# Five tiles' convolution taps on TensorE in four phases, instead of four tiles in two

## What is computed

```python
def conformer_conv_module(x, norm_g, pw1_w, pw1_b, dw_w, dw_b, ln_g, ln_b, pw2_w, pw2_b):
    h = rms_norm(x, norm_g)
    u = h @ pw1_w + pw1_b
    u = u[..., :D_MODEL] * jax.nn.sigmoid(u[..., D_MODEL:])
    u = causal_depthwise_conv(u, dw_w, dw_b)          # 31 taps, each channel by itself
    u = jax.nn.silu(layer_norm(u, ln_g, ln_b))
    return x + u @ pw2_w + pw2_b
```

## Time and profile before

| | us |
|---|---|
| median of 3 runs | 1212.82 |
| lowest, highest | 1211.44, 1214.83 |
| the profiled execution | 1212.73 |
| its span in the profile | 1211.0 |

### The profile page before, as it was taken

The page is one execution under the profiler, slowest core; times in us unless marked ns, Lnnn a source line. Parts: engine busy times, 40 slices in busy tenths (PEclk is TensorE's granted clock), DMA queues, the critical chain, the costliest instruction groups (busy, mean ns, idle before and its releaser), DMA issues.

```text
span 1211.0 us, 16270 instructions
## 1 busy us (share of the span) xinstructions
PE 1188.5 (98%) x6026; PEld 997.4 (82%) x6026; DVE 799.1 (66%) x1099; ACT 506.5 (42%) x814; POOL 62.7 (5%) x76
## 2 busy tenths in 40 slices
PE   8999969999999999999999999999999999999998
PEld 6888838888888888887899999987788888888887
DVE  6998946577527763576667786876677446753763
ACT  6331245444314341334656656655444224421441
POOL 1000001100000000001222021200000000000000
PEclk9999989999999999999999999999999999999999
DMA  8564711232323223222322211231233323332222
GB/s 291 152 125 114 198 46 38 102 100 79 129 76 104 87 89 117 90 87 87 105 71 71 70 42 65 71 105 35 70 104 104 104 70 104 104 104 79 94 78 95
DMA packets 34613, 116.75 MB, mean 96 GB/s; under 512 B 18304, under 2 KB 18432, under 8 KB 21888
## 3 DMA queue, kind: packets, MB, share of 16 engines
q1 hardware_dynamic: 34560, 116.03, 30.3%
HBM read 109.60 MB, written 6.49 MB: 96 GB/s over the span
## 4 chain that ended last, share of the span: by engine, by line
PE 90%; DVE 5%; ACT 3%; issue 1%; DMA 1%; POOL 0%; SPq 0%; POOLq 0%; DVEq 0%; ACTq 0%
PE bank L1240 71%; PE bank L1397 8%; PE bank L1313 5%; PE bank L1447 1%; PE bank L1431 1%; DVE w_lo L839 1%; PE bank L1334 1%; ACT prob L793 1%; PE bank L1304 1%; DVE small L1164 1%; PE bank L1279 1%; DVE dT_lo L1156 1%; DMA w_raw<-stream 1%; PE bank L1416 0%; DVE w_lo L831 0%
## 5 line engine op out<-in xcount | busy, mean ns | idle before, releaser
L1240 PE MATMUL bank<-xg_hi,w_hi 128*128 128x512 f32 x832 | 326.7, 393 | 2.3 <-DVE xg_lo L847 2.3
L1240 PE MATMUL bank<-xg_lo,w_hi 128*128 128x512 f32 x832 | 323.8, 389 | 0.0
L1240 PE MATMUL bank<-xg_hi,w_lo 128*128 128x512 f32 x832 | 323.8, 389 | 0.0
L556 ACT ACTIVATE w_hi<-w_raw 128x2048 fp32r<-128x2048 f32 x79 | 150.6, 1907 | 149.0 <-PE bank L1240 147.1
L831 DVE TENSOR_TENSOR w_lo<-w_raw,w_hi 128x2048 fp32r<-128x2048 f32 x79 | 182.7, 2312 | 31.0 <-ACT w_hi L556 31.0
L1240 PEld LDWEIGHTS bank<-xg_hi,w_hi 128*128 128x128 f32 x832 | 156.2, 188 | 37.0 <-DVE xg_lo L847 2.4
L1240 PE MATMUL bank<-act_hi,w_hi 128*128 128x512 f32 x448 | 177.1, 395 | 7.5 <-DVE act_lo L984 7.2
L708 ACT ACTIVATE ffn_t<-ffn_u,par 128x512 f32<-128x512 f32 x88 | 72.0, 818 | 268.7 <-DVE ffn_u L1054 268.7
L1240 PEld LDWEIGHTS bank<-xg_lo,w_hi 128*128 128x128 f32 x832 | 156.2, 188 | 33.9 <-issue 1.7
L1240 PEld LDWEIGHTS bank<-xg_hi,w_lo 128*128 128x128 f32 x832 | 156.1, 188 | 32.3
L1240 PE MATMUL bank<-act_hi,w_lo 128*128 128x512 f32 x448 | 175.2, 391 | 0.0
(11 more groups left out here) (159 smaller groups left out, 1418.5 us busy)
## 6 DMA issues: line engine op xcount, KB each, us to landing
w_raw<-stream SPq DMA_DIRECT2D x87, 1024.0 KB, 4.9
band_sb<-band SPq DMA_DIRECT2D x12, 512.0 KB, 6.6
w_raw<-stream SPq DMA_DIRECT2D x8, 768.0 KB, 4.1
band<-band_sb SPq DMA_DIRECT2D x4, 1056.0 KB, 12.1
x<-x_t SPq DMA_DIRECT2D x8, 256.0 KB, 6.6
w_raw<-band SPq DMA_DIRECT2D x4, 512.0 KB, 5.8
out_t<-x SPq DMA_DIRECT2D x8, 256.0 KB, 2.0
w_raw<-stream SPq DMA_DIRECT2D x2, 512.0 KB, 5.0
```

The lines of the kernel that those rows point to most:

```text
L556: act.activation(w_hi[:, j, :], w_raw[:, j, :], ACT.Copy).then_inc(w_hi_done, 1)
L1240: got = pe.matmul(out, weights(w, j, k, m), v[:, k, :], start=(k == first and s == 0), stop=(k == last and s == 2), skip_group_check=True)
```

## The change

- **Tiles.** DVE convolves tiles 0 to 2, PE tiles 3 to 7.
- **Phases.** 4 instead of 2: a band is 32 channels by 4 phases, 9 matmuls (OFFSETS) of 128x128, weights 128x1152 (576 KB). There are 20 bands. ACT makes `u2` with 16 copies of 32 partitions by 135 or 136 a tile, and copies a band out with four copies of 32x128.
- **Band rows.** No zero fill of DRAM and no scatter by element. DVE reduces the identity matrix to `taken` (32 columns, which channel of its group a partition is) and makes each tile's rows, 128x992, as tap times `taken` (`make_band`): tiles' rows 0 and 1 in step m = 0 of the pw1 loop, 2 and 3 in m = 1, 4 in m = 2. They go to one of three drafts in SBUF, are stored in DRAM (624 KB, `store_band`), then copied from DRAM to DRAM, four copies of 576 KB a tile, 128 rows of 4608 bytes each (`copy_bands`), and each band is then one load over 128 partitions (`load_band`).
- **Homes.** 13 bands have a place of their own: 3 in `band_sb`, 3 in `w_raw` (free once unit 7 is split), 7 in `xg_band`, which lies over pw1's activations (free when pw1 is done). 7 more reuse places.
- **Queue.** SP's order is new (below), as are the places in which units 8 and 9 are loaded and split.
- **Mean.** DVE adds tiles 0 to 6 into `sq_sum`; PE makes two matmuls with ones instead of eight, one before the last band and one after it.

```diff
-DVE_TILES = [0, 1, 2, 3]
-PE_TILES = [4, 5, 6, 7]
-PHASES = 2
+DVE_TILES = [0, 1, 2]
+PE_TILES = [3, 4, 5, 6, 7]
+PHASES = 4
+CH = P // PHASES
...
+            def store_band(tile):
+                sp.wait_ge(band_made, tile + 1)
+                sp.dma_start(bass.AP(band.tensor, tile * P * BAND, [[BAND, P], [1, BAND]]), drafts[:, tile % DRAFTS, :]
+                             ).then_inc(band_set[tile], 16)
...
+            def copy_bands(tile):
+                sp.wait_ge(band_set[tile], 16)
                 for r in range(PHASES):
...
+                    sp.dma_start(bass.AP(band_rows.tensor, (tile * PHASES * P + r * CH) * BAND_COLS,
+                                         [[BAND_COLS, CH], [P * BAND_COLS, PHASES], [1, BAND_COLS]]),
+                                 bass.AP(band.tensor, tile * P * BAND + r * CH, [[BAND, CH], [CH * BAND, PHASES], [1, BAND_COLS]])
+                                 ).then_inc(band_copied[tile], 16)
+
+            def load_unit(n):
+                sp.wait_ge(w_lo_done, n - RING + 1)
+                sp.dma_start(w_raw[:, n % RING, :], stream[:, STARTS[n]:STARTS[n + 1]]).then_inc(w_in[n % RING], 16)
+
+            load_unit(2)
+            load_unit(3)
+            load_unit(4)
+            store_band(0)
+            store_band(1)
+            copy_bands(0)
+            load_unit(5)
+            copy_bands(1)
+            store_band(2)
+            store_band(3)
+            copy_bands(2)
+            copy_bands(3)
+            load_unit(6)
+            store_band(4)
+            copy_bands(4)
+            load_unit(7)
+            for n in range(HOMES):
+                if n % PHASES == 0:
+                    sp.wait_ge(band_copied[n // PHASES], 16 * PHASES)
+                if n == SB_BANDS:
+                    sp.wait_ge(w_lo_done, KT)
+                if n == SB_BANDS + RAW_BANDS:
+                    sp.wait_ge(tiles, TILE0 + 2 * KT)
                 load_band(n)
...
+            def make_band(tile):
+                dve.wait_ge(taken_set, 1)
+                dve.wait_ge(band_edges, 2)
+                if tile >= DRAFTS:
+                    dve.wait_ge(band_set[tile - DRAFTS], 16)
+                dve.tensor_tensor(drafts[:, tile % DRAFTS, BAND_AT:BAND_AT + TAPS * CH].rearrange("p (t c) -> p t c", c=CH),
+                                  p("dw_w", PE_TILES[tile] * TAPS, TAPS).rearrange("p (t c) -> p t c", c=1).broadcast_to([P, TAPS, CH]),
+                                  taken.rearrange("p (t c) -> p t c", t=1).broadcast_to([P, TAPS, CH]),
+                                  ALU.mult).then_inc(band_made, 1)
...
+                for tile in {0: (0, 1), 1: (2, 3), 2: (4,)}.get(m, ()):
+                    make_band(tile)
                 convolve(4)
                 if 0 < m < KT - 2:
                     split_weights(m + 2, j)
...
-            convolve(12)
-            split_weights(KT + 1, 1)
-            convolve(len(taps))
+            dve.wait_ge(c_done, len(DVE_TILES))
+            for n in range(KT - 2):
+                if n:
+                    dve.wait_ge(conv_summed, n)
+                if n + 1 in PE_TILES:
+                    dve.wait_ge(band_out, PHASES * (n + 2 - PE_TILES[0]))
+                if n == len(DVE_TILES) + 1:
+                    split_weights(KT + 1, 1)
+                dve.tensor_tensor(sq_sum, sq_sum if n else conv_c[:, 0, :], conv_c[:, n + 1, :], ALU.add).then_inc(conv_summed, 1)
```

More of the change, by code:

```diff
@@ L52 @@
 CHUNKS = [KT, KT, FT - 2 * KT]
-DVE_TILES = [0, 1, 2, 3]
-PE_TILES = [4, 5, 6, 7]
-PHASES = 2
+DVE_TILES = [0, 1, 2]
+PE_TILES = [3, 4, 5, 6, 7]
+PHASES = 4
+CH = P // PHASES
+OFFSETS = (TAPS + PHASES - 2) // PHASES + 1
+BAND_COLS = OFFSETS * P
+BAND = (OFFSETS * PHASES + PHASES - 1) * CH
+PHASE_SEQ = SEQ // PHASES
+PHASE_COLS = PHASE_SEQ + OFFSETS - 1
+BANDS = PHASES * len(PE_TILES)
 FIRST_PARAMS = 3 * KT
 WARM = 14
[L61 to L65, removed]
+RAW_BANDS = 3
+SB_BANDS = 3
+XG_BANDS = 7
+BAND_AT = (PHASES - 1) * CH
+DRAFTS = 3
+HOMES = SB_BANDS + RAW_BANDS + XG_BANDS
+AGAIN = [n for n in range(HOMES) if not SB_BANDS <= n < SB_BANDS + RAW_BANDS]
 PARAM_WIDTHS = [
@@ L205, in trunk @@
         x, at = put("x", top, [P, KT, SEQ])
+        xg_band, _ = put("xg_band", at, [P, XG_BANDS * BAND_COLS])
         xg_hi, at = put("xg_hi", at, [P, KT, SEQ], F32R)
@@ L263, in trunk @@
         ln_sq, at = put("ln_sq", at, [P, 2, SEQ])
-        band_sb, at = put("band_sb", at, [P, 2 * SLOT])
-        zeros = band_sb[:, 2 * SLOT - BAND:2 * SLOT]
+        band_sb, at = put("band_sb", at, [P, max(SB_BANDS * BAND_COLS, DRAFTS * BAND)])
+        drafts = band_sb[:, 0:DRAFTS * BAND].rearrange("p (n c) -> p n c", n=DRAFTS)
+        taken, at = put("taken", at, [P, CH])
         neg_mean = conv_a[:, 0, :]
@@ L333, in trunk @@
         c_done = sem("c_done")
[L334 to L337, removed]
+        taken_set = sem("taken_set")
+        band_edges = sem("band_edges")
+        band_made = sem("band_made")
+        band_set = [sem(f"band_set{n}") for n in range(len(PE_TILES))]
+        band_copied = [sem(f"band_copied{n}") for n in range(len(PE_TILES))]
+        band_in = [sem(f"band_in{n}") for n in range(HOMES)]
         band_used = sem("band_used")
@@ L343, in trunk @@
         mean_mm = sem("mean_mm")
+        conv_summed = sem("conv_summed")
         xc_done = sem("xc_done")
@@ L392, in band_slot, with band_last @@
         def band_slot(n):
-            return n if n < 2 else 2 + n % 2
+            return n if n < HOMES else AGAIN[(n - HOMES) % len(AGAIN)]
         def band_home(n):
-            return w_raw[:, n, 0:SLOT] if n < 2 else band_sb[:, (n % 2) * SLOT:(n % 2 + 1) * SLOT]
+            at = band_slot(n)
+            if at < SB_BANDS:
+                home = band_sb
+            elif at < SB_BANDS + RAW_BANDS:
+                home, at = w_raw.rearrange("p j c -> p (j c)"), at - SB_BANDS
+            else:
+                home, at = xg_band, at - SB_BANDS - RAW_BANDS
+            return home[:, at * BAND_COLS:(at + 1) * BAND_COLS]
         def band_count(n):
-            return 32 if n < 2 else 32 * (n // 2)
+            return 16 * sum(band_slot(i) == band_slot(n) for i in range(n + 1))
+        def band_last(n):
+            return max(i for i in range(n) if band_slot(i) == band_slot(n))
         block = ctx.enter_context(nc.Block())
@@ new lines, in _ @@
+            load_unit(6)
[9 more added lines that the diff above has]
+                    sp.wait_ge(tiles, TILE0 + 2 * KT)
+                load_band(n)
+            n = HOMES
+            while n < BANDS:
+                if n % PHASES == 0:
+                    sp.wait_ge(band_copied[n // PHASES], 16 * PHASES)
+                sp.wait_ge(band_used, band_last(n) + 1)
+                load_band(n)
+                n += 1
+                if n == HOMES + SB_BANDS:
+                    for j in range(RING):
+                        sp.wait_ge(band_used, SB_BANDS + 2 + j)
+                        sp.dma_start(w_raw[:, j, :], stream[:, STARTS[KT + j]:STARTS[KT + j + 1]]).then_inc(w_in[j], 16)
@@ L617, in _ @@
                 if m in PE_TILES:
-                    act.wait_ge(pad_done, 1)
-                    n = 2 * (m - PE_TILES[0])
-                    for h in range(2):
+                    act.wait_ge(pad_done, 2)
+                    n = PHASES * (m - PE_TILES[0])
+                    for g in range(PHASES):
                         for r in range(PHASES):
-                            got = act.activation(u2[r * HD:(r + 1) * HD, n + h, :],
-                                                 conv_u[h * HD:(h + 1) * HD, m, r:CP:PHASES], ACT.Copy)
+                            at = conv_u[g * CH:(g + 1) * CH, m, r:CP:PHASES]
+                            got = act.activation(u2[r * CH:(r + 1) * CH, n + g, 0:at.shape[-1]], at, ACT.Copy)
                     got.then_inc(u_split, 1)
@@ L629, in _ @@
             for n in range(BANDS):
[L630 removed]
+                tile, g = divmod(n, PHASES)
                 act.wait_ge(band_used, n + 1)
                 for e in range(PHASES):
[L633 to L634 removed]
+                    got = act.activation(conv_c[g * CH:(g + 1) * CH, PE_TILES[tile], e:SEQ:PHASES],
+                                         bank[CONV[n % len(CONV)]][(PHASES - 1 - e) * CH:(PHASES - e) * CH, 0:PHASE_SEQ], ACT.Copy)
                 got.then_inc(band_out, 1)
[L636 removed]
+                if n in (8, 11):
                     split_weights(KT + n % 2, n % 2)
@@ L955, in _ @@
             own.mark(dve.tensor_scalar(gsub, p("subln_g"), 1.0 - LAM_INIT, None, ALU.mult))
-            convolve(16)
+            convolve(len(taps))
             split_weights(KT, 0)
@@ L1300, in _, with mean @@
                     unit(2 * i + j, j, xg_hi, xg_lo, KT)
-            def mean(m, start=False, stop=False):
-                return pe.matmul(bank[NORM][:, :], ones[:, :], conv_c[:, m, :], start=start, stop=stop, skip_group_check=True)
+            def mean(v, start=False, stop=False):
```

(15 more changed lines are left out.)

22 lines of the change are left out of this document (8 added, 14 removed).

## The result

The changed kernel takes **1220.11 us** (median of 4 runs, 1219.12 to 1221.92) against 1213.53 for the kernel before in the same runs: a ratio of 1.0058, 95% interval 1.0038 to 1.0077. It is slower by 0.6%, where 0.6% faster was forecast. The profiled execution took 1219.12 us, its span is 1217.3, 6.3 more than before. What was to get cheaper got cheaper: TensorE (PE) is busy 12.6 us less. It waits more.

A forecast was written before the change was run, and what follows sets the result against it. TensorE was taken as the bound, VectorE nearly so in pw1. Band stretch -15.8, VectorE in pw1 +4.15 and SP's queue +4.2 gave -7.4 us against 1212.73: 1205 us, range 1199 to 1222.

The forecast's parts named there:

- Bands on PE: TensorE's band matmuls: 360 records at 0.112 us, 40.3 us, instead of 256 longer ones.
- warm-up rival: Band matmuls: short ones stay at 0.19 us a record as in warm-up, 28 us more, 1233; chance 2%.
- DVE in pw1: VectorE in pw1: the reduction and five make_band delay units 3 and 4, +4.15 us.
- The 0.9 us at unit 4: VectorE in pw1: the fifth make_band, before unit 4's low part, makes it 0.9 us later still.
- SP's queue: Loads of units 5 to 7 behind stores and copies; unit 7 late, +4.2 us.
- R: Rate of DRAM to DRAM copies in SP's queue, in MB per us: taken as 0.36.
- rival 3: Queue copies pass each byte twice, R 0.215, units 6 and 7 starve TensorE: 1223; most of slower's 23%.
- rival 2: Queue copies at R about 0.28 cancel the gain: 1212.7, within 0.3% for R 0.26 to 0.31; chance 13%.
- ACT: ScalarE: tile 7's copies 5.3 us, a band's way out 1.25; PE stalls 3.1 us before band 3.
- End of the bands: After the last band: its bare way out, then one mean of 0.97, 2.4 us together.
- +-2 on the sum: Whole kernel: allowance in us for where half-clock stretches fall; one over 3.4 us of matmuls costs 1.7.
- -7.4: Whole kernel: forecast change in us, summed from -15.8, +4.15 and +4.2.

The follow-up runs named there:

- e1: Changed kernel with units 6 and 7 loaded earlier in SP's queue, ahead of copies of later tiles: 1209.24 us, ratio 0.9975 to the kernel before.
- e4: Changed kernel with u copies reading and bands' way out writing contiguous columns, no 16-byte step (computation altered): 1211.45 us.
- e2: Changed kernel with tile 7's 16 copies of u made by GpSimd instead of ScalarE: 1210.37 us, ratio 0.998 to the kernel before.
- e5: Changed kernel with ten taps moved out of the pw1 loop to behind it, make_band staying on VectorE: 1216.61 us, ratio 1.0031 to the kernel before.
- e8: Changed kernel with each DRAM to DRAM copy reading and writing 128 adjoining rows of 4608 bytes (bands hold other numbers): 1219.66 us.
- e3: Changed kernel with make_band on GpSimd and the reduction at VectorE's start: 1222.47 us, ratio 1.0088 to the kernel before.

## Why the prediction was wrong, point by point

- **Bands on PE: right.** 54 records take 6.19 us with 0.28 for one: (6.19 - 0.28) / 53 = 0.1115 us, forecast 0.112. The warm-up rival fell.
- **DVE in pw1: right in its place, with its clock left out.** The five rows took 1.18 us each in the trace, 1.10 start to start, and unit 3 started 3.3 us later than the forecast's 44.65 (3.2 forecast). Not in the sum was the half clock behind the wait (1.5 us). The 0.9 us at unit 4 did not appear, since PE was late by more than that.
- **SP's queue: the mechanism right, its price too low; a step that failed.** In the sum unit 7's weights land at 66.1 + 26.2 = 92.3 us; they landed at 97.8. The waits of units 6 and 7 are 4.7 and 1.8 by starts, and the half clock behind the first 2.5: 9.0 us where 4.2 stood. The forecast took R = 0.36, "the upper two thirds of the way" between two rows. The sum's formula, 9.44 MB / R - 22.0 us, gives 9.0 with R = 0.305, near the 0.302 of 62 to 78 us. That agreement is in part luck: this stretch holds a pause that the sum counts apart, and without it R is 0.339 (64 to 76 us), which gives 5.8, and it is 0.415 for 3 us of tile 1's copies. How the 4.8 us divide between rate and pauses is not shown; no single R describes the copies. The page HBM Reference of the Trainium skill (Specifications) gives the 716 GB/s from which the prediction estimated 0.358 for R; the trace does not agree, with 0.415 at its fastest, which is over it, and 0.325 from 66 to 76 us. Nor does it agree with the 0.207 to 0.214 of the page DMA: Bandwidth & Descriptors of the Trainium skill (Latency and other measured facts). Half of the one-way rate, which is rival 3, fell with it. The loss of 9.0 us lies in rival 2's span (R from 0.26 to 0.31).
- **ACT: the step that failed most.** "So about 0.29 to 0.31 for 128, and 0.33 for the 135 of a copy" took the price per element of contiguous rows and of steps of 8 bytes for one with 16 bytes. Measured: 7.28 us for tile 7's copies, not 5.3 (+2.0), 1.63 for a band's way out, not 1.25 (+0.4). And they started 4.4 us into the bands, not 2.64 (+1.8): tile 7's sigmoid had to wait for ACT, still copying tile 6. That last part is no error of the price alone. It took the late units and the long copies together, since the copies start at 2.64 both in e1, where the units are in time, and in e4, where the copies are short. Half clock behind the wait: +1.5. PE's stall was 7.3 + 1.5 us where 3.1 was in the sum. e2 shows it: without the stall 9.7 us are back, and e4 shows that the sum was right but for the price: 2.92 for 3.1.
- **End of the bands: right**, 2.8 us for 2.4.
- **The clock.** "I put +-2 on the sum" was one-sided in truth: the change made three waits of over 3 us in a stretch where PE had none, each with a stretch of half clock behind it, 5.5 us in all. A wait of this length should have been priced with it, but as a range: the same wait of 3.0 us at unit 3 cost 1.5 us here and 3.1 in e2, whose stretch is this (columns as above):

```profile
46.60:53.40 6.80, 6.14 (x15) 4.84 (x15) 6.80 (x11) 2.31 (x2) 0.00 (x0) 0.50 0.81 297
```

Together: queue +4.8, ACT before band 3 +5.7, the clock at unit 3 +1.5 less unit 4's 0.9, the end of the bands 0.4, norm and beyond 1.1. From -7.4 this makes +5.2; measured is +6.4 between the two profiled executions. A microsecond stays unassigned. These parts are read by starts and are not independent: e5 removed the 4.8 us of unit 3 and the first band came 2.5 us earlier. The result lies inside the range. The sign was wrong because two terms that no row priced, the copies' rate and the step of 16 bytes, were both taken near their cheap end, and because no wait was priced with its half clock.

## What to carry to other kernels

A change that shortens the busiest engine's work pays only if what feeds and empties it keeps the new pace: price the feeders' instructions at their new access step, and ask when the engine that drains the first result comes free, not only how long it takes. On a queue that drains in order, put the loads that the busy engine waits for ahead of bulk traffic that is wanted later; here this alone was worth 10 to 11 us. Count each new wait of the matmul engine with the half clock that may follow it, half of what it then does at that level. In pw1 and the bands of these runs the waits of 3.02 to 7.90 us cost 1.5 to 3.1 us each in this way, and not in the order of their length; the waits of 2.80 (e2) and 2.92 us (e4) cost nothing behind them.

## What the hardware showed that I had not expected

- ScalarE pays 0.9 ns an element contiguous or at a step of 8 bytes, and 1.8 at 16 bytes (e4), for reads and, by the same 0.9 ns more, for writes.
- DRAM to DRAM copies of 4608-byte rows ran at 410 to 415 GB/s for 2 to 3 us (53 to 56, 64 to 66) and at 325 from 66 to 76 us; a load behind such copies ran at 287. Layout of the source and size of the packets, changed together, made no difference (e8, 338 against 339 GB/s).
- GpSimd work with SBUF operands delays VectorE instruction by instruction: beside a multiplication of two operands a 128x2048 subtraction took 3.95 us instead of 2.29, and a 128x512 multiply-add 2.35 instead of 0.75 (e3); beside plain copies in e2 a tap took 0.91 instead of 0.74.
- PE's waits of 3.05, 4.55 and 7.30 us were each followed or overlapped by a granted clock of 0.50; that of 1.65 us was not, nor e4's of 2.92.
